# Two more pairs of projection blocks by seven products for eight, in a two-layer fp32 decoder trunk

## The reference

```python
h = rms_norm(x, pre_g)
proj = h @ w_in               # 2048 x (12 * 1536 + 3 * 2048): the sections below
# attention q,k,v,z   conv u,b,c,z   retention q,k,v,z   merge gates g_a,g_c,g_r
o_a = dilated_mixture_attn(q_a, k_a, v_a) * silu(z_a)
o_c = b_c * causal_short_conv(c_c * u_c, conv_w, conv_b) * silu(z_c)
o_r = retention(q_r, k_r, v_r) * silu(z_r)
merged = (sigmoid(g_a) * (o_a @ w_branch_a) + sigmoid(g_c) * (o_c @ w_branch_c)
          + sigmoid(g_r) * (o_r @ w_branch_r))
x = x + rms_norm(merged @ w_out, post_g)
```

## Time and profile before

| | |
|---|---|
| median of three runs | 2713.33 us (2712.95 to 2714.37) |
| the profiled execution, its own time | 2712.87 us |
| its span, first to last instruction | 2711.0 us |
| PE busy | 2699.1 us, 12120 matmuls |
| DVE busy | 1881.8 us |
| ACT busy | 1308.4 us |
| DMA | 579.43 MB, mean 214 GB/s |

### The profile page before, as it was taken

How to read it: one execution, slowest core, us unless ns; L and a number is a source line. 1 busy time by engine, 2 the same in 40 slices (tenths; PEclk the granted TensorE clock), 3 DMA queues, 4 the chain that set the end, 5 groups by cost and what they waited for, 6 DMA issues and landing times.

```text
span 2711.0 us, 30218 instructions
## 1 busy us (share of the span) xinstructions
PE 2699.1 (100%) x12120; PEld 2240.9 (83%) x12120; DVE 1881.8 (69%) x2102; ACT 1308.4 (48%) x1504; POOL 29.4 (1%) x42
## 2 busy tenths in 40 slices
PE   9999999999999999999999999999999999999998
PEld 7888888888888888888878888888888888888887
DVE  6656775888865666678576567658888656666884
ACT  6454554555543344454454545545555433444543
POOL 0000000000000000000000000000000000000000
PEclk9999999999999999999999999999999999999999
DMA  9677466665666676656576674657656656766563
GB/s 333 212 226 232 163 229 198 230 203 192 228 233 197 206 241 209 217 207 222 178 235 206 217 241 155 235 185 233 226 189 221 234 191 215 233 214 218 202 222 120
DMA packets 299291, 579.43 MB, mean 214 GB/s; under 512 B 12304, under 2 KB 37264, under 8 KB 298896
## 3 DMA queue, kind: packets, MB, share of 16 engines
q1 hardware_dynamic: 260976, 517.50, 56.9%
q10 hardware_dynamic: 37168, 55.13, 7.0%
q0 software_dynamic: 1008, 4.87, 0.5%
HBM read 548.10 MB, written 29.36 MB: 213 GB/s over the span
## 4 chain that ended last, share of the span: by engine, by line
PE 98%; DMA 1%; SPq 1%; DVE 0%; ACT 0%; issue 0%; POOL 0%; DVEq 0%; POOLq 0%
PE ps L928 29%; PE ps L930 29%; PE ps L929 29%; PE ps L895 3%; PE ps L894 3%; PE ps L893 3%; DMA raw<-w_in 0%; SPq L734 0%; PE ps L839 0%; PE ps L837 0%; PE ps L836 0%; PE ps L815 0%; PE ps L819 0%; DMA merged<-xT 0%; PE ps L801 0%; PE ps L820 0%
## 5 line engine op out<-in xcount | busy, mean ns | idle before, releaser
L1269 DVE TENSOR_TENSOR w_trail<-raw,w_lead 128x1024 fp32r<-128x1024 f32 x1045 | 1265.2, 1223 | 770.4 <-ACT w_lead L1002 767.3
L1002 ACT ACTIVATE w_lead<-raw 128x1024 fp32r<-128x1024 f32 x1045 | 1101.7, 1060 | 1250.0 <-PE ps L930 1120.7
L928 PE MATMUL ps<-w_lead,hT_lead 128*128 128x512 f32 x2944 | 1149.4, 390 | 2.1 <-DVE w_trail L1612 1.0
L930 PE MATMUL ps<-w_lead,hT_trail 128*128 128x512 f32 x2944 | 1145.6, 389 | 0.0
L929 PE MATMUL ps<-w_trail,hT_lead 128*128 128x512 f32 x2944 | 1145.5, 389 | 0.0
L928 PEld LDWEIGHTS ps<-w_lead,hT_lead 128*128 128x128 f32 x2944 | 552.7, 188 | 118.1 <-issue 3.6
L930 PEld LDWEIGHTS ps<-w_lead,hT_trail 128*128 128x128 f32 x2944 | 552.6, 188 | 115.0
L929 PEld LDWEIGHTS ps<-w_trail,hT_lead 128*128 128x128 f32 x2944 | 552.8, 188 | 113.5
L928 PE MATMUL ps<-w_lead,oT_lead 128*128 128x512 f32 x576 | 224.2, 389 | 0.0
L930 PE MATMUL ps<-w_lead,oT_trail 128*128 128x512 f32 x576 | 224.1, 389 | 0.0
L929 PE MATMUL ps<-w_trail,oT_lead 128*128 128x512 f32 x576 | 224.1, 389 | 0.0
(11 more groups left out here) (130 smaller groups left out, 1158.9 us busy)
## 6 DMA issues: line engine op xcount, KB each, us to landing
raw<-w_in SPq DMA_DIRECT2D x381, 1024.0 KB, 5.2
raw<-w_out SPq DMA_DIRECT2D x32, 1024.0 KB, 5.1
raw<-w_branch_a SPq DMA_DIRECT2D x24, 1024.0 KB, 5.2
raw<-w_branch_c SPq DMA_DIRECT2D x24, 1024.0 KB, 5.2
raw<-w_branch_r SPq DMA_DIRECT2D x24, 1024.0 KB, 5.4
bounce_q<-vq_sb ACTq DMA_DIRECT2D x18, 512.0 KB, 3.5
vq_sb<-bounce_q ACTq DMA_DIRECT2D x72, 128.0 KB, 4.1
bounce_z<-z_sb ACTq DMA_DIRECT2D x18, 512.0 KB, 4.0
```

The source lines that it names most:

```text
L928: pe.matmul(acc, lead[:, k, tok(t)], wl, start=opens, stop=False)
L930: last = pe.matmul(acc, trail[:, k, tok(t)], wl, start=False, stop=closes)
L1002: act.activation(w_lead[:, (l * HALVES + h) % SPLIT_SLOTS, :], raw[:, SLOT_OF[l, i][0], part:part + HALF * COLS], ACT.Copy).then_inc(lead_ ...
L1269: dve.tensor_tensor(w_trail[:, s, :], raw[:, SLOT_OF[l, i][0], part:part + HALF * COLS], w_lead[:, s, :].bitcast(F32), ALU.subtract).then_ ...
```

## The change

Attention's roles are taken in the order q, k, z, v. In groups 1 and 2 of both layers q and k are a pair, by seven products for eight; that adds four pairs to twelve. The pair's results arrive in `q_sb` and `k_sb` unscaled, evicted by DVE, so ACT scales them in place (`q_scale`, `k_scale`, two activations of 128x512 each) before they are sent. The exponential is taken in two halves of two heads; its output goes to a spare area (in `gates`), from there to DRAM and back (`p0_away`, `p0_back`, `p1_away`, `p1_back`: 384 KB each way), and four DVE transposes of 128x384 finish it, in place of the sixteen of 32x384. The maxima are taken for two heads at a time. The last weight sum of every pair (`q4`) is made two units later. The side work of attention is now counted from block z, the third of a group:

| attention, group 0 / 1, after the change | step or unit |
|---|---|
| ACT: q_scale, q_away | 18 / 56 |
| ACT: q_back, k_scale, k_away | 20 / 58 |
| ACT: k_back | 22 / 60 |
| DVE: transposes of q, of k | 23, 24 / 61, 62 |
| PE: scores, behind unit | 21 / 59 |
| DVE: scores; ACT: both exp and away | 25, 26 / 63, 64 |
| ACT: p0_back, p1_back; DVE: p0, p1 | 29, 30, 31, 32 / 67 to 70 |
| PE: values, behind unit; DVE: values | 39, 43 / 77, 81 |
| ACT: z_away, z_back, out; DVE: z, out | 45, 48, 53; 52, 54 / 83, 86, 91; 90, 92 |

Block z of group 0 begins at unit 16, the pair of group 1 at unit 32, block z of group 1 at unit 54, the pair of group 2 at unit 70. The eviction of the pair's q is DVE's at step 55 (93 for group 2).

```diff
-ROLES = {"attention": "vqkz", "conv": "zbuc", "retention": "vqkz"}
+ROLES = {"attention": "qkzv", "conv": "zbuc", "retention": "vqkz"}
...
-               + [first_block("conv", g) + 2 for g in range(GROUPS)])
+               + [first_block("conv", g) + 2 for g in range(GROUPS)]
+               + [first_block("attention", g) for g in range(1, GROUPS)])
...
-SUMS = {"q5": (1, "p1"), "p7": (3, None), "p6": (5, "q5"), "q4": (9, "p6")}
+SUMS = {"q5": (1, "p1"), "p7": (3, None), "p6": (5, "q5"), "q4": (10, "p6")}
...
+COUNTED_FROM = {"attention": 2, "conv": 0, "retention": 0}
...
+                h = unit_after(first_block(mixer, g) + COUNTED_FROM[mixer], at)
+                out.setdefault(h + offset, []).append((what, mixer, g))
...
-    "attention": [("scores", 4 * B), ("values", 5 * B + 3)],
+    "attention": [("scores", 5), ("values", 2 * B + 4.5)],
...
-    "attention": [("q_away", 2 * B - 1), ("q_back", 2 * B + 1), ("k_away", 3 * B - 1), ("k_back", 3 * B + 1),
-                  ("exp", 4 * B + 1), ("z_away", 5 * B + 4), ("z_back", 6 * B + 4), ("out", 6 * B + 6.5)],
+    "attention": [("q_scale", -2), ("q_away", -2), ("q_back", 0), ("k_scale", 0), ("k_away", 0), ("k_back", 2),
+                  ("exp0", 6), ("p0_away", 6), ("exp1", 6), ("p1_away", 6), ("p0_back", 9), ("p1_back", 10),
+                  ("z_away", 2 * B + 6), ("z_back", 2 * B + 8), ("out", 2 * B + 11)],
...
-    "attention": [("q", 2 * B + 4), ("k", 3 * B + 4), ("scores", 4 * B), ("sums", 4 * B + 2)]
-                 + pieces("probs", 4 * B + 3) + [("values", 5 * B + 3), ("z", 6 * B + 6), ("out", 6 * B + 7)],
+    "attention": [("q", 3), ("k", 4), ("scores", 5), ("sums", 7), ("p0", 11), ("p1", 12),
+                  ("values", 2 * B + 4.5), ("z", 2 * B + 10.5), ("out", 2 * B + 12)],
...
-VALUES_LATE = 4
-for _n in [first_block("attention", g) for g in range(1, GROUPS)]:
-    EVICT_DUE[LAST_HALF[_n] + AHEAD + VALUES_LATE] = EVICT_DUE.pop(LAST_HALF[_n] + AHEAD)
...
+        spare = gates[:, 0, 0:HPB * 3 * P].rearrange("p (s c) -> p s c", s=2)
...
+                    act.wait_ge(*turned(l, "q", mixer, j - 1))
+                    act.wait_ge(*turned(l, "k", mixer, j - 1))
+                elif
...
+                if what in ("p0", "p1"):
+                    part = int(what[1])
+                    act.wait_ge(exp_ready, HPB * (l * GROUPS + g) + HPB // 2 * (part + 1))
+                    act.dma_start(bounce[what], spare[:, part]).then_inc(away[what], 16)
+                    return
...
-                elif what == "exp":
-                    act.wait_ge(neg_max_ready, l * GROUPS + (g + 1))
-                    for h in range(HPB):
-                        for t, cols in ((0, slice(0, P)), (1, slice(P, 3 * P))):
+                elif what in ("q_scale", "k_scale"):
+                    n = role_block(mixer, what[0], g)
+                    if n in PAIR_OF:
+                        tile, done = {"q": (q_sb, q_scaled), "k": (k_sb, k_scaled)}[what[0]]
+                        act.wait_ge(*moved_out(l, n))
+                        for t in range(TILES):
+                            act.activation(quads(tile, t), quads(tile, t), ACT.Copy,
+                                           scale=x_rstd[:, t:t + 1]).then_inc(done, 1)
+                elif what in ("exp0", "exp1"):
+                    part = int(what[-1])
+                    if l > 0 and g == 0 and part == 0:
+                        act.wait_ge(residual_out, l * (16 * OUT_BLOCKS))
+                    act.wait_ge(neg_max_ready, 2 * (l * GROUPS + g) + part + 1)
+                    by_quarter = spare[:, part].rearrange("p (j h c a) -> p h c j a", j=QUADS, h=HPB // 2, c=3)
+                    for h in range(HPB // 2 * part, HPB // 2 * (part + 1)):
+                        for t, tiles in ((0, slice(0, 1)), (1, slice(1, 3))):
                             c = TILES * h + t
-                            last = act.activation(probs[:, h, cols], probs[:, h, cols], ACT.Exp,
+                            taken = probs[:, h, tiles.start * P:tiles.stop * P]
+                            last = act.activation(by_quarter[:, h % (HPB // 2), tiles],
+                                                  taken.rearrange("p (c j a) -> p c j a", j=QUADS, a=SQ), ACT.Exp,
                                                   bias=neg_max[:, c:c + 1]
...
+                        if h % 2:
+                            two = slice(h - 1, h + 1)
+                            for i in range(h - 1, h + 1):
+                                dve.wait_ge(*step_drained(l, STEP["scores", mixer, g, i]))
+                            by_tile = neg_max.rearrange("p (h t) -> p h t", t=TILES)
+                            dve.tensor_reduce(by_tile[:, two, 0], probs[:, two, 0:P], AX_X, ALU.max, negate=True)
+                            dve.tensor_reduce(by_tile[:, two, 1], probs[:, two, P:3 * P], AX_X, ALU.max,
+                                              negate=True).then_inc(neg_max_ready, 1)
...
+            def turn(l, what, mixer, g):
+
+                part = int(what[1])
+                if part == 0:
                     before = l * 3 * GROUPS + group_no[mixer, g]
                     if before > 0:
                         dve.wait_ge(out_trail, TILES * before)
-                    dve.wait_ge(exp_ready, l * (HPB * GROUPS) + HPB * (g + 1))
-                a, b = TURNS[piece]
-                for n in range(a, b):
-                    i, j = n // QUADS, n % QUADS
-                    rows = src[SQ * i:SQ * (i + 1), :, :].rearrange("p h (c x) -> p h c x", c=3)
-                    turned_to = dst[SQ * j:SQ * (j + 1), :, :].rearrange("p h (c x) -> p h c x", c=3)
-                    last = dve.transpose(turned_to[:, :, :, SQ * i:SQ * (i + 1)], rows[:, :, :, SQ * j:SQ * (j + 1)])
-                last.then_inc(done, 1)
+                dve.wait_ge(back[what], 16 * QUADS * trips(l, what, mixer, g))
+                squares = spare[:, part].rearrange("p (i h c a) -> p h c i a", i=QUADS, h=HPB // 2, c=3)
+                for h in range(HPB // 2):
+                    last = dve.transpose(probsT[:, HPB // 2 * part + h, :].rearrange("p (c i b) -> p c i b", c=3, i=QUADS),
+                                         squares[:, h])
+                last.then_inc(probs_turned, 1)
```

More of the change, by code:

```diff
@@ L101, in branch_block, with role_block @@
     return BLOCK_NO["branch", mixer, "", j]
+def role_block(mixer, role, g):
+    return BLOCK_NO["mix", mixer, role, g]
 def first_block(mixer, g):
@@ L385, in build @@
     bounce = {what: nc.dram_tensor(f"bounce_{what}", (P, TILES * COLS), F32).ap() for what in ("q", "k", "z")}
+    for what in ("p0", "p1"):
+        bounce[what] = nc.dram_tensor(f"bounce_{what}", (P, HPB // 2 * 3 * P), F32).ap()
     x_rows = x.rearrange("(t p) d -> p t d", p=P)
@@ L500, in build @@
         conv_joined = sem("conv_joined")
-        away = {what: sem(what + "_away") for what in ("q", "k", "z")}
-        back = {what: sem(what + "_back") for what in ("q", "k", "z")}
+        away = {what: sem(what + "_away") for what in ("q", "k", "z", "p0", "p1")}
+        back = {what: sem(what + "_back") for what in ("q", "k", "z", "p0", "p1")}
+        q_scaled = sem("q_scaled")
+        k_scaled = sem("k_scaled")
         q_turned = sem("q_turned")
@@ L596, in turned @@
             if what == "probs":
-                return probs_turned, len(TURNS) * (l * GROUPS + g + 1)
+                return probs_turned, 2 * (l * GROUPS + g + 1)
             if what == "prod":
@@ L605, in trips @@
         def trips(l, what, mixer, g):
+            if what in ("p0", "p1"):
+                return l * GROUPS + g + 1
             if what == "k":
@@ L616, in gate_sigmoids, with scaled @@
             return gate_ready, TILES * (2 * (l * len(GATE_PAIRS) + GATE_PAIRS.index(PAIR_OF[n])) + n - PAIR_OF[n] + 1)
+        def scaled(l, role, g):
+            return {"q": q_scaled, "k": k_scaled}[role], TILES * (l * (GROUPS - 1) + g)
         def pair_tile(n, i, t):
-            kind, _mixer, _role, j = BLOCKS[n][3]
+            kind, mixer, _role, j = BLOCKS[n][3]
             if kind == "gate":
                 return gates[:, t, COLS * (j + i):COLS * (j + i + 1)]
-            return quads((v_sb, q_sb)[i], t)
+            return quads((v_sb, q_sb)[i] if mixer == "conv" else (q_sb, k_sb)[i], t)
         def in_order(n, ap):
@@ L1011, in evict @@
                                ("conv", "b"): k_sb}.get((mixer, role))
-                    if copy_to is not None:
+                    if copy_to is not None and n not in PAIR_OF:
                         act.wait_ge(*done_block(l, n))
@@ L1052, in pair_copy @@
                 act.wait_ge(*done_product(l, what, n))
-                if what == "p1" and kind == "mix" and j == 0:
+                if what == "p1" and kind == "mix" and mixer != "conv":
+                    act.wait_ge(*turned(l, "q", mixer, j - 1))
+                    act.wait_ge(*turned(l, "k", mixer, j - 1))
```

(12 more changed lines are left out.)

41 lines of the change are left out of this document (16 added, 25 removed).

## The result

| | before | after |
|---|---|---|
| median of 4 runs | 2713.58 us (2712.95 to 2714.37) | 2761.03 us (2759.43 to 2762.44) |
| ratio after to before | | 1.0175, 95% interval 1.0157 to 1.0192 |
| profiled execution, own time | 2712.87 us | 2762.39 us |
| its span | 2711.0 us | 2760.5 us |
| mean granted clock of TensorE | 0.999 | 0.991 |

A forecast was written before the change was run, and what follows sets the result against it. PE was taken as the bound, with 98% of the chain. Terms of -10.9 + 2.2 + 10.4 + 1.6 = +3.3 us gave a median of 2716.6 us, with an 8-in-10 range of 2706 to 2728.

The forecast's parts named there:

- the floor of 1.1 us: PE's wait at every attention scores from the order of steps and units alone, wake-up included: 1.1 us each.
- a clock below 1.00 as a sign of being wrong: In the profile after, PE's granted clock below 1.00 would show the forecast wrong; no size was given.
- 12 matmuls less in four pairs: q and k of groups 1 and 2, two layers: 180 matmuls for 192 per pair, 10.9 us off PE.
- scores' wait, the two groups 0: PE waits 1.1 us for k's transposes at the scores of each group 0, 2.2 us in all.
- scores' wait, groups 1 and 2: Scores of groups 1 and 2: ACT's splits stand behind the trips; PE waits 2.6 us four times, 10.4 us.
- eviction before block z: Block z of groups 1 and 2 waits for DVE's eviction of the pair's q: 0.4 us four times, 1.6.
- k's way out meeting q's return: k_away leaves during q's return, which would push the wait to the upper figure, about 5 us each for 2.6.
- the mean of all traffic over z and v (262 GB/s): DMA load in z and v, 8.4 + 2.1 + 1.6 MB in 46 us: 262 GB/s for a mean of 214.
- My third rival: Trips land late among weights, returns and probabilities, each us of landing costing up to 8: 2719 to 2730, chance 0.25.
- My upper figure: Scores of groups 1 and 2, with 4.5 us for both ways out: waits of about 5 us each.
- the DVE sums and splits: Each new pair adds DVE sums (9.1 us) and splits (7.3); PE covers such work in conv pairs, so no cost.
- The q4 sum: The later q4 sum moves 2.2 us of DVE by two units: no wait in any of the twelve old pairs.

The follow-up runs named there:

- The small trips: Kernel after the change, attention's q and k trips cut to 16 of 1024 columns (8 KB for 512): 2720.65 us, ratio 1.0027.
- Trips apart from each other: Kernel with scores four units later, k sent before the wait for q, returns and DVE's transposes later: 2707.61 us, ratio 0.9981.
- the busy matmuls in the wait: Kernel after the change, with twenty extra 128x512 matmuls before PE's wait at each of attention's scores: 2741.14 us, ratio 1.0103.
- the last experiments: Scores four units later and q and k trips apart, plus z's transposes and trail later: 2703.73 us; with q4's sum two units earlier again: 2704.67 us.

## Why the prediction was wrong

Right was that PE would wait at all six scores for k's transposes, and for groups 1 and 2 the reason, ACT's splits behind the trips. Three steps failed: groups 0 got only the floor of 1.1 us, without the trips; the landings in groups 1 and 2 were priced too low; and the clock behind the waits was in no term. The prediction had named a clock below 1.00 as a sign of being wrong, and the profile of after shows it, 0.991 in the mean.

| step of the forecast | forecast, us | measured, us |
|---|---|---|
| 12 matmuls less in four pairs | -10.9 | -10.9 (12072 matmuls) |
| scores' wait, the two groups 0 | +2.2 | +13.4 |
| scores' wait, groups 1 and 2 | +10.4 | +25.8 |
| scores at the low clock | in no term | +13.7 |
| eviction before block z | +1.6 | +1.9 |
| start, matmuls behind the scores, end, spread | in no term | +5.6 |
| sum | +3.3 | +49.5 |

**Groups 0: the floor taken for the whole.** I gave them 1.1 us each, as if only the order of units and steps counted. But k_away and q_back are in ACT's program there too. The ACT queue of group 0, layer 0:

```profile
55.45 0.34 ACTq L1128 DMA_DIRECT2D bounce_q<-vq_sb  x1
61.21 1.78 ACTq L1140 DMA_DIRECT2D vq_sb<-bounce_q  x4
63.03 0.45 ACTq L1128 DMA_DIRECT2D bounce_k<-k_sb  x1
68.97 1.76 ACTq L1140 DMA_DIRECT2D k_sb<-bounce_k  x4
```

The same chain holds them, with ways out of 5.76 and 5.94, and PE waits 7.13. What I had worked out for groups 1 and 2 should have been worked out here.

**Groups 1 and 2: landings.** The chain itself was the right one. Its marks from the start of q_scale, in group 1 of layer 0 (152.54):

| | forecast | measured |
|---|---|---|
| q_away issued | 1.2 | 1.4 |
| q_back may issue | 4.8 | 6.2 |
| k_away issued | 7.8 | 9.4 |
| k_back may issue | 11.2 | 13.3 |
| issued | 13.0 | 15.1 |
| k turned | 18.9 | 21.9 |

Less the 16.3 of six units, that leaves 5.6, and PE waited 5.5. Of the 3.0 us too little, 1.8 are the two ways out, and 0.8 is k's own return, which I had left out of the chain, since with 4.4 us it landed before it was needed. I had priced both by the medians of the earlier trace rows, of trips far from each other. The traffic explains the difference in direction: the window over q's way out shows 306 GB/s, and a DMA share of 0.89, where over q's way out of the same group in before it shows 207 and 0.74. The window of after, then that of before:

```profile
153.90:158.70 4.80, 4.80 (x23) 3.97 (x22) 3.30 (x4) 2.13 (x2) 0.00 (x0) 1.00 0.89 306
```

```profile
145.90:149.40 3.50, 3.50 (x18) 2.88 (x16) 1.35 (x2) 1.33 (x3) 0.00 (x0) 1.00 0.74 207
```

What differs is the weights. On their queue, q1, 0.94 MB pass in the window of after and 0.20 MB in that of before (packets, MB, share):

```profile
q1 hardware_dynamic: 478, 0.94, 62.3%
```

```profile
q1 hardware_dynamic: 98, 0.20, 14.7%
```

The other queue of these windows, q10, moves 0.52 MB in both, which is q's trip alone. So it was not in the main, as I had argued, k's way out meeting q's return: in groups 1 and 2 k's ways out took 3.9, 4.5, 2.9 and 3.1 us, and q's, with no return under way, 4.8, 3.8, 6.2 and 6.7. The prediction had taken the mean of all traffic over z and v (262 GB/s); from 140.0 to 152.5, just before q leaves, the trace shows 372. That the weights made the landings long is read from this one trace; no run moved them.

The small trips show that the bytes of these trips count (waits down by 26.9). Trips apart from each other were tried only once the scores were late, where they brought no measurable gain; at the places of after it wasn't tried. My third rival had this mechanism, trips that land late among the weights, with 1 us of landing at 8 us of time, but stopped at 5 us a group.

The sentence that I quoted against the forecast (the Trainium skill, DMA: Bandwidth & Descriptors, "Issuing engines are not separate DMA queues") says that DMAs of all issuing engines run on the same 16 engines. The trace agrees: q's way out, on ACT's queue, was slower where SyncE's queue moved more beside it. I set the rule aside for the trace's quiet medians, though those were no rows of the state that the change makes. My upper figure, about 5 us a group, was nearer to the measured 5.5, 5.5, 7.1 and 7.7, but rested on the wrong meeting.

**The clock.** I had the rule (the Trainium skill, TensorE: Matmul & The Clock Gate, "Why this matters for your kernels": idle gaps between bursts bring the slow clock back) and put it aside because no row of before shows a fall. Before has no long wait: its longest, at the start, is 1.8 us. A trace with no long wait can't speak against a rule on long waits. The trace of after agrees with the rule: 0.50 in the window behind the wait, and 13.7 us for it; the busy matmuls in the wait took 11.7 of that away.

**The eviction before block z** came out as worked, 0.47 us four times. That it could be removed by placing z later, the last experiments show. And the DVE sums and splits, costed at nothing beside the pairs, are free: no wait of PE inside the new pairs' products is among those listed for after. The q4 sum is free too.

Open are 1.3 us spread over the program and the 2.4 in the first 30 us. The 2.4 need not come from the change: four other versions with the four pairs lost only 0.1 to 0.6 there. Landings in layer 1 are longer at the same places (q's 6.2 and 6.7 us in groups 1 and 2, k's 8.9 in group 0). More weights pass beside them, 1.3 to 1.9 MB; why the weights fall there is open as well.

## What to carry to other kernels

When work that waits for a landing is moved into an engine's program, work out for every group, not only the changed ones, what stands behind it. Price its landings by rows with the traffic that the change itself makes; where there are none, take the long ones. Price a wait of some microseconds of TensorE at its length plus the slower burst behind it, and look for a place some units later before giving up the change: here the same edits lost 47 us at one place and gained 9.4 at another.

## What the runs showed of the hardware

- The granted clock was 0.50 for all or part of a burst of 2.43 us behind long idle times: the scores took 3.7 to 4.9 us in all 20 bursts behind 2.5 to 7.7 us, and 2.51 in the 16 behind 2.4 us and less. A longer idle time did not mean a slower burst (4.4 us behind 7.1, 4.9 behind 5.5). In the 4.7 us after the burst of group 1, layer 0, the clock was 0.96, then 1.00.
- DMAs of 8 KB took nearly as long to land as 512 KB in quiet: medians of 2.3 (k) and 3.8 us (q) against 2.8 and 3.5. Nine of these twelve had 145 to 253 GB/s of weights beside them and took 2.5 to 5.4 us; the two with 10 GB/s or less took 1.4 and 1.7. The 512 KB took from 2.9 to 8.9 us in one kernel.
- The four DMA issues of a return, 128 KB each, held ACT's queue for 1.76 us at the least and in most cases, and up to 3.3. In the version with the trips apart, whose returns of q go out right behind k's way out, they held it for 2.5:

```profile
148.51 0.34 ACTq L1128 DMA_DIRECT2D bounce_k<-k_sb  x1
...
148.92 2.52 ACTq L1140 DMA_DIRECT2D vq_sb<-bounce_q  x4
```
